# Recurrent heads, attention and Fourier mixing of a layer in one stage, with the recurrence's outputs in token rows

## The chip, the cores and the metric

The kernel runs on one core of one Trainium2 chip, in float32 throughout. The metric is the device time of one execution in microseconds (us). The matrix products are done by TensorE (PE in the profile; PEld is its weight load), element-wise work by VectorE (DVE), functions such as exp by ScalarE (ACT), and SyncE (SP) issues the weight transfers.

## The reference, cut to what matters

The network is two blocks. The first has two layers (`DEPTH = 2`) over 256 context and 256 latent tokens, width 1024; the second block is one layer and isn't touched by the change. A layer of the first block projects the normed tokens with one wide matrix and gives the columns to three branches, which are then merged:

```python
ul, uc = _split_cols(hl @ w_in), _split_cols(hc @ w_in)
ml_l, ml_c = _mlstm_branch(ul, uc, ml_gate_b, ml_head_g)
da_l, da_c = _diff_attn_branch(ul, uc, da_lam, da_head_g, cos, sin, lam_init, need_ctx)
yl = _merge(ml_l, da_l, _fourier(ul[8]), ul[9], w_br_ml, w_br_da, w_br_fn, w_out)
```

- The recurrence (mLSTM, 4 heads of 256): for both directions of time, with gate sums b and running maxima m, weights exp(min(bc + g, 0)) times q·k under a causal mask; the output of a direction is (weights @ v) / max(|sum of weights|, exp(-m)). The two directions are added, normed over the head's 256 channels, and multiplied with a gain and sigmoid(o).
- Differential attention (8 heads, a pair of them per 256 columns): two softmaxes per head with axial rotary positions, the second one subtracted with a factor, times v, normed per head.
- Fourier mixing (4 groups of 256 channels): the real part of a 2-D FFT over the tokens of a stream and the channels of a group:

```python
y = jnp.fft.fftn(z, axes=(1, 3), norm='ortho').real
```

In the second layer only the latent tokens' output is needed (`need_ctx` false), but keys and values of all tokens are.

## The kernel before, in words

Activations lie in SBUF as channels on partitions by tokens: `c.h` (normed) and `c.big` (the branches' outputs, 24 tiles of 128 channels). Weights come through a ring of four slots of 1 MB (1024 rows by 256 columns), each loaded by SyncE once the slot's last reader is through. PSUM has eight banks of 512 columns. The code is a row of stages (`Core.stage`). Within a stage each engine runs its own list and waits for others by semaphores; at a stage's end all engines meet (L228, `PEq L228` in the rows), and the semaphores are cleared. `full` is true in the first layer (`lo = 0`, all 512 tokens give outputs), false in the second (`lo = 256`).

Three functions make the branches of a layer, one after the other.

`mlstm` (L656) works head by head through `staggered` (L635): a stage of `projections` of a head and a stage of `core`, in turns, as a loop over three heads. `projections` (L763) multiplies K, Q and O with tokens last (16 multiplies of 8 by 8 tiles, L782), V with tokens first (L807), and beside them VectorE and ScalarE end the head before: |denominator|, maximum, reciprocal of 512 columns (L817, L818), product, sum over directions, squares, a multiply with ones over channels (L793), and the norm (L828 to L835). The first head's stage also holds `Gates`: gate products (L687), log-sigmoid, scans over tokens (L731 to L742), and the turned gate columns (L695). `core` (L875) does scores (L884), `A` on VectorE and ScalarE, and outputs with channels on partitions (L892): two multiplies with v and one with ones (the denominator) for each source tile.

`diff_attention` (L924) is a single stage, written out without loops. `steps` gives the order: while the items (a head by 128 tokens: scores L1046, exp L1101, `combine`, transposes L1059, output L1071, sums L1079) of a pair are worked off, the eight projection jobs of the next pair (L1015, L1021, with the quarter turns of the rotary positions, L1034) stand between them on TensorE. The first pair's jobs have no items beside them, and the last pair's items no jobs.

`fourier` (L1221) is a stage per group, three of them in a loop: projections with tokens last (L1236), a product with cosine and sine over channels (512 columns per token tile, L1243), a product over tokens (L1252), a copy into `c.big`.

After that comes `tail` (L1414 is its product), the same before and after.

Of the kernel before, what the change touches and what calls it, by code (L numbers as in the profile page):

```python
# [17 lines left out]
ALU = mybir.AluOpType  # L18
ACT = mybir.ActivationFunctionType
# [22 lines left out]
ML_COLUMNS, DA_COLUMNS, FN_COLUMNS = (COL_Q, COL_K, COL_O, COL_V), (COL_DAQ, COL_DAK, COL_DAV), (COL_FN,)  # L42
# [34 lines left out]
def _constant_columns():  # L77
    at = 0
    for name, width in (("ident", P), ("ones", P), ("upper", P), ("lower", P), ("turn", P), ("cos", NLAT), ("sin", NLAT),
                        ("dft", 2 * 3 * FN_C), ("pick", 4 * HG_SUB - 1), ("inner", HG_HEADS * NLAT), ("iota", PEER_K)):  # L80
        CST[name] = (at, width)
        at += width
    return at
# [25 lines left out]
class Core:  # L109


    def __init__(self, nc, ctx):
# [23 lines left out]
        def sem(name):  # L136
# [33 lines left out]
        self.decayed = sem("decayed")  # L170
        self.da_roped = sem("da_roped")
# [17 lines left out]
                     self.cleared, self.merged, self.averaged, self.inverted, self.rooted, self.scaled, self.moved, self.carried, self.paired, self.scored, self.apart,  # L189
                     self.decayed, self.da_roped, self.da_scored, self.da_max, self.da_exp, self.da_mixed, self.da_turned,  # L190
# [423 lines left out]
def over_turns(c, turns, columns, w_in, body, following):  # L614


    if not c.fetched:
        with c.stage() as block:
            @block.sync
            def _(sp):  # L620
                fetch(c, sp, head_loads(w_in, columns, 0))
    had = list(c.ahead_n)

    def wait_loaded(turn):
        return lambda engine, s: engine.wait_ge(c.ahead[s], turn * 16 + 16 * had[s])

    with c.nc.Fori(0, turns - 1) as turn:
        body(turn, wait_loaded(turn),
             lambda sp, wait_free=None: fetch(c, sp, head_loads(w_in, [col + CHUNK for col in columns], turn), wait_free))
    for s in range(len(columns)):  # L630
        c.ahead_n[s] = had[s] + turns - 1
    body(turns - 1, wait_loaded(turns - 1), lambda sp, wait_free=None: fetch(c, sp, following, wait_free))


def staggered(c, turns, columns, w_in, projections, core, following):  # L635


    if not c.fetched:
        with c.stage() as block:
            @block.sync  # L640
            def _(sp):
                fetch(c, sp, head_loads(w_in, columns, 0))
    had = list(c.ahead_n)

    projections(0, None, lambda engine, s: engine.wait_ge(c.ahead[s], 16 * had[s]))
    with c.nc.Fori(0, turns - 1) as turn:
        core(turn, lambda sp: fetch(c, sp, head_loads(w_in, [col + CHUNK for col in columns], turn)))
        projections(turn + 1, turn, lambda engine, s: engine.wait_ge(c.ahead[s], turn * 16 + 16 * (had[s] + 1)))
    for s in range(len(columns)):
        c.ahead_n[s] = had[s] + turns - 1  # L650
    core(turns - 1, lambda sp: fetch(c, sp, following))
    projections(None, turns - 1, None)


def mlstm(c, a, layer, w_in, full, following):
# [4 lines left out]
    lo = 0 if full else NCTX  # L660
    n = T - lo
    gcol, gh, headg, q, k, v, o, bc, A0, A1, E, den, hs, sq = c.carve(
        (2 * 4, 4), (2 * 4,), (2,), (2, T), (2, T), (4, ML_D), (2, T), (4, T), (4, T), (4, T), (2, T), (2, T), (2, T), (2, T))
    *_, gates, b, g, m, out_rows, wg, wg_apart = c.carve(
        (2 * 4, 4), (2 * 4,), (2,), (2, T), (2, T), (4, ML_D), (2, T), (4, T), (4, T), (2, T), (2, T), (2, T), (4, T), (KT, 16),
        (KT, P))
    logf, e = out_rows[:, 0:2], out_rows[:, 2:4]
    H = ML_HEADS

    class Gates:  # L670

        @staticmethod
        def sync(sp):
            sp.dma_start(wg, w_in[:, :, COL_GATE:COL_GATE + 16]).then_inc(c.stored, 16)

            sp.wait_ge(c.vec_out, 3)
            sp.wait_ge(c.act_out, 5)
            sp.dma_start(a["rows"], out_rows[0:H]).then_inc(c.stored, 16)  # L680
            sp.wait_ge(c.stored, 32)

        @staticmethod
        def products(pe):
            pe.wait_ge(c.drained, 1)
            for k in range(KT):
                last = pe.matmul(c.banks[7][:], wg_apart[:, k, :], c.h[:, k, :], start=k == 0, stop=k == KT - 1)  # L687
            last.then_inc(c.turned, 1)

        @staticmethod  # L690
        def turn(pe):
            pe.wait_ge(c.vec_out, 1)
            for d in range(2):
                for j in range(4):
                    last = pe.matmul(c.banks[6][:, (4 * d + j) * 4:(4 * d + j + 1) * 4], g[0:H, d, j * P:(j + 1) * P],  # L695
                                     c.constant("ident")[0:H, 0:H], start=True, stop=True)
            last.then_inc(c.turned, 1)
            pe.wait_ge(c.vec_out, 3)
# [2138 lines left out]
```

## Time and profile before

| | us |
|---|---|
| median of 3 runs | 3744.62 (3741.59 to 3747.61) |
| the profiled execution | 3744.39 |
| its span, first to last instruction | 3742.5 |
| TensorE busy | 3312.4 (89%) |
| VectorE busy | 1571.2 (42%) |
| ScalarE busy | 703.1 (19%) |

Shares of busy time are means over the whole span. The rows further down cut it into stretches. A float32 multiply shows as two records and two weight loads, so an "x32" is 16 multiplies. The granted clock is 1.0 at 2.4 GHz and 0.5 at 1.2 GHz; in a stretch it is the mean.

### The profile page before, as it was taken

The page shows a single profiled execution, that of the slowest core. Times are in us where ns is not written, and L with a number is a line of the kernel's source. Part 1 is how long each engine was busy: PE and PEld are TensorE (multiplying, and loading weights), DVE is VectorE, ACT ScalarE, POOL GpSimd, SP SyncE. Part 2 cuts the span into 40 slices and gives each one's busy share as a digit, 9 for nine tenths or more (in the row PEclk, how much of TensorE's full clock was granted, in tenths as well). Part 3 has the DMA queues.
Part 4 walks back from the last instruction along what each step waited for, and adds up shares of the span by engine and source line. Part 5 has one row for each costly group of instructions (what it writes and reads, how often), then busy time and mean ns, then how long its engine had stood idle before and what let it go on. Part 6 is the DMA issues. An engine that isn't in the chain of part 4 may idle for free. (4 is left out here: it accounts for less than half of the span.)

```text
span 3742.5 us, 33417 instructions
## 1 busy us (share of the span) xinstructions
PE 3312.4 (89%) x11640; PEld 2040.9 (55%) x11640; DVE 1571.2 (42%) x3286; ACT 703.1 (19%) x1639; POOL 426.7 (11%) x568
## 2 busy tenths in 40 slices
PE   6999799689999999998998978999989777787887
PEld 2555455344444844466766646888877663332332
DVE  1433345514432320002333443745127237777775
ACT  1211123300000200002111220010022104444443
POOL 0000000000000000000000000000000006665664
PEclk9999899799999999999999989999998789898989
DMA  5111110016433342232312203459432229999998
GB/s 183 68 56 56 66 58 23 1 34 224 148 133 124 137 155 79 76 99 79 113 67 80 67 1 121 153 179 373 150 124 68 68 71 424 422 416 411 410 423 351
DMA packets 280265, 588.69 MB, mean 157 GB/s; under 512 B 10888, under 2 KB 238984, under 8 KB 240584
## 3 DMA queue, kind: packets, MB, share of 16 engines
q0 software_dynamic: 44160, 338.97, 22.1%
q1 hardware_dynamic: 235984, 248.08, 19.9%
q8 instruction: 79, 1.29, 0.1%
q14 instruction: 42, 0.34, 0.0%
HBM read 585.91 MB, written 1.11 MB: 157 GB/s over the span
## 5 line engine op out<-in xcount | busy, mean ns | idle before, releaser
L1414 PE MATMUL banks<-normed,weight_ring 128*128 128x256 f32 (+1 forms) x2272 | 708.4, 474 | 9.1 <-ACT normed L1651 3.8
L1414 PEld LDWEIGHTS banks<-normed,weight_ring 128*128 128x128 f32 x2272 | 434.4, 191 | 281.1 <-issue 240.3
L1414 PE MATMUL banks<-branches,weight_ring 128*128 128x256 f32 (+1 forms) x1648 | 477.4, 451 | 0.0
L1414 PEld LDWEIGHTS banks<-branches,weight_ring 128*128 128x128 f32 x1648 | 313.1, 190 | 162.0 <-issue 133.9
L2677 PE MATMUL banks<-weight_ring,work 128*128 128x512 f32 x512 | 282.6, 711 | 127.5 <-ACT work L2642 127.5
L782 PE MATMUL banks<-normed,weight_ring 128*128 128x512 f32 (+1 forms) x768 | 282.6, 528 | 26.5 <-PEq L228 26.5
L2677 PEld LDWEIGHTS banks<-weight_ring,work 128*128 128x128 f32 x512 | 113.3, 229 | 296.2 <-issue 238.1
L2677 PE MATMUL banks<-work 128*128 128x512 f32 x512 | 229.4, 596 | 13.2 <-ACT work L2642 13.0
L546 DVE CUSTOM_DVE_ANT_0 work<-work 128x1024 f32<-128x1024 f32 x176 | 205.2, 1222 | 83.9 <-DMA work<-ada_turned 76.4
L782 PEld LDWEIGHTS banks<-normed,weight_ring 128*128 128x128 f32 x768 | 146.8, 192 | 157.2 <-issue 150.6
L1015 PE MATMUL banks<-normed,weight_ring 128*128 128x512 f32 (+1 forms) x512 | 205.7, 558 | 20.5 <-PEq L228 14.0
L2595 DVE CUSTOM_DVE_ANT_0 work<-work,branches 128x1024 f32<-128x1024 f32 x128 | 156.1, 1229 | 98.8 <-DMA work<-experts,work 95.7
L2677 PEld LDWEIGHTS banks<-work 128*128 128x128 f32 x512 | 95.3, 190 | 143.2 <-issue 104.0
L2570 POOL COPY work<-branches 128x1 uint32 (+1 forms) x256 | 114.8, 449 | 499.5 <-POOLq L228 466.5
L1015 PEld LDWEIGHTS banks<-normed,weight_ring 128*128 128x128 f32 x512 | 98.4, 196 | 122.8 <-issue 109.5
L2595 DVE CUSTOM_DVE_ANT_0 weight_ring<-weight_ring,branches 128x1024 f32<-128x1024 f32 x128 | 150.8, 1224 | 28.8 <-DMA weight_ring<-experts,work 22.8
L2574 POOL DMA_INDIRECT weight_ring<-experts,work x128 | 141.6, 1106 | 109.0 <-POOL work L2570 68.2
L2574 POOL DMA_INDIRECT work<-experts,work x128 | 141.8, 1108 | 101.9 <-POOL work L2570 80.4
L1551 DVE SCALAR_TENSOR_TENSOR stream<-banks,modulation,stream 128x256 f32<-128x256 f32 x48 | 22.7, 483 | 287.8 <-PE banks L1414 287.8
L1603 DVE TENSOR_TENSOR branches<-banks,branches 128x512 f32<-128x512 f32 (+1 forms) x44 | 24.1, 557 | 262.7 <-PE banks L1414 262.6
L1021 PE MATMUL banks<-weight_ring,normed 128*128 128x256 f32 x512 | 117.0, 383 | 4.2 <-DVE work L1144 4.2
L516 POOL DMA_DIRECT2D work<-condition_rows x2 | 1.2, 623 | 1040.5 <-issue 876.8
(408 smaller groups left out, 3739.3 us busy)
## 6 DMA issues: line engine op xcount, KB each, us to landing
weight_ring<-w_in SPq DMA_DIRECT2D x98, 1024.0 KB, 5.1
work<-ada_turned POOLq DMA_DIRECT2D x41, 1536.0 KB, 8.2
weight_ring<-w_ffn_in SPq DMA_DIRECT2D x44, 1024.0 KB, 5.1
weight_ring<-w_ffn_out SPq DMA_DIRECT2D x20, 1024.0 KB, 4.8
weight_ring<-w_out SPq DMA_DIRECT2D x12, 1024.0 KB, 4.8
weight_ring<-w_ada_first SPq DMA_DIRECT2D x8, 1024.0 KB, 8.7
work<-rows SPq DMA_DIRECT2D x8, 1024.0 KB, 4.7
weight_ring<-w_br_ml SPq DMA_DIRECT2D x8, 1024.0 KB, 5.3
```

Source lines behind the costliest of these rows:

```text
L516: pool.dma_start(self.rows[:, lo:hi, :], self.a["condition_rows"][lo:hi].partition_broadcast(P)).then_inc(c.rows_loaded, 16)
L546: last = dve.tensor_tensor_reduce(out=out, in0=slot[:, t, :], in1=self.rows[:, row, :], scale=1.0, scalar=0.0, op0=ALU.mult, op1=ALU.add, ...
L782: last = pe.matmul(c.banks[bank + half][:, 0:T - first], c.ring[:, s, kk, half * P:(half + 1) * P], c.h[:, kk, first:T], start=kk == 0, st ...
L1015: last = pe.matmul(bank[:, first:T], w[:, kk, half * P:(half + 1) * P], c.h[:, kk, first:T], start=kk == 0, stop=kk == KT - 1)
L1021: last = pe.matmul(bank[:, 0:2 * P], c.h[:, kk, j * P:(j + 1) * P], w[:, kk, :], start=kk == 0, stop=kk == KT - 1)
L1414: ins = pe.matmul(bank(i)[:, in_bank(p0, p1)], w[:, k - at, half * P:(half + 1) * P], source[:, k, cols(p0, p1)], start=k == 0, stop=k == ...
L1551: dve.scalar_tensor_tensor(out, bank(i + t)[:, in_bank(p, p + 1)], mod[:, gate_tile + t, parts[p][2]:parts[p][2] + 1], out, ALU.mult, ALU. ...
L1603: dve.tensor_tensor(out, bank(B_UP + NF + j)[:, in_bank(0, wide)], out, ALU.mult).then_inc(c.drained, 1)
L2570: pool.tensor_copy(place_u[:, r:r + 1], experts_u[:, bass.ds(u * K + (q * R + r), 1)]).then_inc(c.pool_done, 1)
L2574: pool.indirect_dma_start(out=fetched[r], out_offset=None, in_=a["experts"], in_offset=bass.IndirectOffsetOnAxis(ap=place_u[:, r:r + 1], a ...
L2595: dve.tensor_tensor_reduce(out=urows[r], in0=urows[r], in1=tokens[:, t, :], scale=1.0, scalar=0.0, op0=ALU.mult, op1=ALU.add, accum_out=do ...
L2677: last = pe.matmul(c.banks[2 * t + half][:], diag[:, r, :], vrows[r][:, half * 512:(half + 1) * 512], start=first, stop=isinstance(u, int) ...
```

## The change

The functions `over_turns`, `staggered`, `mlstm`, `diff_attention` and `fourier` go, and one function `branches` holds a single stage for all three branches of a layer, written out without loops. Its order on TensorE:

```python
for number in range(ML_JOBS):
    ml_job(0, number)
    if number == 1:
        gate_products()
    if number == 5:
        gate_turn()
for head in range(H):
    for step in range(ML_JOBS):
        if step < 4:
            ml_scores(head, step)
        if head + 1 < H:
            ml_job(head + 1, step)
        elif step < DA_JOBS:
            da_job(0, step)
        ml_after(head, step)
for item, kind, pair, number in da_steps():
    if item is not None and item < items:
        scores(item)
    if kind == "da":
        da_job(pair, number)
    if kind == "fn":
        fn_job(number)
    if item == items:
        turn_tokens(0)
    if item is not None:
        turn(item - 1)
    if item == items:
        turn_tokens(1)
    if item is not None:
        if ends_half(item - 2):
            output(item - 2)
        if item == items + 2:
            turn_channels(0)
        if ends_half(item - 3):
            sums(item - 3)
turn_tokens(2)
turn_channels(1)
turn_tokens(3)
turn_channels(2)
turn_channels(3)
```

A job is one bank: 0 to 5 are the halves of K, Q and O, 6 to 9 the four token tiles of V. All projections use banks 6 and 7 in turn and each job waits until the bank of two jobs before is copied; the recurrence's buffers are doubled. `ml_after` starts at step 3 (full) or 5 (`OUT_STEP`), and does the transposes of the tile before, then the outputs of this one. The recurrence's outputs are now in token rows, with the denominator as the 257th column of v:

```diff
-                for d in range(2):
-                    pe.wait_ge(c.vec_out, 4 * (d + 1))
-                    for bank, lhs in zip(outputs[d], (0, 1, None)):
-                        for i, (j, a0, a1) in enumerate(runs[d]):
-                            weights = c.constant("ones") if lhs is None else v[:, j, lhs * P:(lhs + 1) * P]
-                            pe.matmul(c.banks[bank][:, a0 - lo:a1 - lo], weights, A[d][:, j, a0:a1], start=i == 0,
-                                      stop=i == len(runs[d]) - 1)
+                for d in range(2):
+                    js = sources(d, t)
+                    for j in js:
+                        last = pe.matmul(c.banks[2 + 2 * (done % 2) + d][:, 0:V_W], A[d][:, j, t * P:(t + 1) * P], ml_v[buf][:, j, :],
+                                         start=j == js[0], stop=j == js[-1])
+                last.then_inc(c.ml_out, 1)
...
+    def sources(d, t):
+        if d == 0:
+            return list(range(t + 1))
+        return list(range(t, 2)) if t < 2 else [0, 1] + list(range(t, 4))
```

The norm of a tile is then a chain over per-token values, and two transposes bring it back to channels on partitions:

```diff
+            def join(head, x):
...
+                for d in range(2):
+                    chain.mark(dve.tensor_copy(its[:, d:d + 1], both[d][:, ML_D:V_W]))
+                chain.wait()
+                chain(dve.scalar_tensor_tensor(its[:, 0:2], its[:, 0:2], -1.0, its[:, 0:2], ALU.mult, ALU.max))
+                chain(dve.tensor_tensor(its[:, 0:2], its[:, 0:2], ecol[:, t:t + 5:4, head], ALU.max))
+                chain(dve.reciprocal(its[:, 2:4], its[:, 0:2]))
+                chain(dve.tensor_scalar(out, both[0][:, 0:ML_D], its[:, 2:3], None, ALU.mult))
+                dve.scalar_tensor_tensor(out, both[1][:, 0:ML_D], its[:, 3:4], out, ALU.mult, ALU.add).then_inc(c.ml_joined, 1)
...
+            def ml_square(head, x):
+                act.activation(squares, hs[done % 2], ACT.Square, accum_out=stat[:, done % 2, 4:5]).then_inc(c.ml_squared, 1)
...
+            def ml_invert(head, x):
+                chain(dve.tensor_scalar(its[:, 4:5], its[:, 4:5], 1.0 / ML_D, EPS, ALU.mult, ALU.add))
+                dve.reciprocal(its[:, 5:6], its[:, 4:5]).then_inc(c.ml_inverted, 1)
...
+            def ml_level(head, x):
+                act.activation(stat[:, done % 2, 6:7], stat[:, done % 2, 5:6], ACT.Sqrt).then_inc(c.ml_rooted, 1)
+                act.activation(hs[done % 2], hs[done % 2], ACT.Copy, scale=stat[:, done % 2, 6:7]).then_inc(c.ml_leveled, 1)
...
+                for half in range(2):
+                    last = pe.transpose(c.banks[2 + 2 * (done % 2)][:, half * P:(half + 1) * P],
+                                        hs[done % 2][:, half * P:(half + 1) * P], c.constant("ident"))
+                last.then_inc(c.ml_turned, 1)
```

`ml_place` then multiplies gain and sigmoid(o) into `c.big`. The gates' work is spread between the first head's copies on VectorE (`gate_fold`, `gate_sums` and `gate_maxima` ahead of copies 2, 3 and 4), and the turn (`gate_turn`) now also turns exp(-m) and waits for it (`gate_raised`), since the maximum is taken per token.

Fourier's projections are now tokens first (two token tiles to a bank), and the transforms come in the other order and use the symmetry of cosine and sine: over tokens with 129 cosine and 127 sine columns, over channels with 128 outputs of each kind, one more weight tile for the middle frequency, and the mirrored half made by adding and subtracting on VectorE (`fn_place`):

```diff
+                    for half in range(2):
+                        for kk in range(2):
+                            last = pe.matmul(c.banks[2 * (group % 2) + s][:, half * FN_C:(half + 1) * FN_C],
+                                             z[group][:, 2 * s + kk, half * P:(half + 1) * P], over_tokens[:, kk, :],
+                                             start=kk == 0, stop=kk == 1)
...
+                for half in range(2):
+                    last = pe.matmul(x_bank[:, used], over_channels[:, half, 0], uv[:, 2 * half, used], start=half == 0, stop=half == 1)
+                last.then_inc(c.fn_even, 1)
+                for half in range(2):
+                    pe.matmul(y_bank[:, used], over_channels[:, half, 1], uv[:, 2 * half + 1, used], start=half == 0, stop=False)
+                for half in range(2):
+                    last = pe.matmul(y_bank[:, used], over_channels[:, half, 2], uv[:, 2 * half, used], start=False, stop=half == 1)
```

`used` is 258 columns wide in the first layer and 129 in the second. ScalarE copies the token transform out of PSUM (`fn_spread`, four copies a group in the first layer) and lifts the even part (`fn_lift`). The constants change with it, and the rows of `w_br_fn` are put in the new channel order on the host when the inputs are packed. `ML_COLUMNS` has K before Q.

## Rows read from the trace of the kernel before

**Rows 1.** The page: the engine's busy time; weight loads of one line, mean ns.

```profile
PE 3312.4 (89%) x11640; PEld 2040.9 (55%) x11640; DVE 1571.2 (42%) x3286; ACT 703.1 (19%) x1639; POOL 426.7 (11%) x568
L782 PEld LDWEIGHTS banks<-normed,weight_ring 128*128 128x128 f32 x768 | 146.8, 192 | 157.2 <-issue 150.6
```

**Rows 2.** Windows: start:end, length, busy us by engine, granted clock, DMA.

```profile
74.70:142.85 68.15, 65.99 (x192) 35.80 (x193) 17.49 (x28) 12.42 (x14) 0.00 (x0) 0.97 0.06 18
142.85:385.17 242.32, 228.64 (x703) 129.27 (x703) 96.66 (x145) 34.27 (x55) 0.00 (x0) 0.99 0.19 65
385.17:478.37 93.20, 69.11 (x210) 39.91 (x211) 36.90 (x60) 10.04 (x16) 0.00 (x0) 0.85 0.20 68
478.37:675.43 197.06, 183.74 (x644) 105.16 (x643) 103.07 (x214) 56.81 (x136) 0.00 (x0) 0.98 0.12 38
675.43:874.95 199.52, 155.16 (x424) 81.53 (x423) 58.80 (x96) 23.76 (x55) 0.00 (x0) 0.87 0.11 37
1735.50:1795.82 60.32, 54.68 (x193) 37.15 (x193) 17.00 (x28) 11.93 (x14) 0.00 (x0) 0.93 0.07 20
1795.82:1978.69 182.87, 170.04 (x684) 129.04 (x685) 61.77 (x133) 27.00 (x55) 0.00 (x0) 0.98 0.25 86
1978.69:2048.43 69.74, 55.03 (x204) 40.31 (x204) 25.24 (x56) 8.07 (x16) 0.00 (x0) 0.88 0.27 91
2048.43:2195.17 146.74, 140.50 (x550) 93.75 (x549) 68.01 (x144) 37.59 (x76) 0.00 (x0) 1.00 0.16 51
2195.17:2318.72 123.55, 87.38 (x294) 58.60 (x293) 34.57 (x62) 15.05 (x32) 0.00 (x0) 0.83 0.16 52
```

**Rows 3.** TensorE's timeline over one head, first layer: start, us, instruction, [idle before].

```profile
164.04 13.99 PE L782 MATMUL banks<-normed,weight_ring 128*128 128x512 f32 x32 [1.06 <-PEq L228]
...
177.87 1.88 PE L793 MATMUL banks<-work,constants_sb 128*128 128x512 f32 x4
...
207.05 13.98 PE L807 MATMUL banks<-weight_ring,normed 128*128 128x256 f32 x64
223.16 5.41 PE L884 MATMUL banks<-work 128*128 128x512 f32 x16 [2.13 <-PEq L228]
230.03 4.58 PE L892 MATMUL banks<-work 128*128 128x512 f32 x16 [1.46 <-DVEq L918]
...
244.33 13.99 PE L782 MATMUL banks<-normed,weight_ring 128*128 128x512 f32 x32 [1.06 <-PEq L228]
```

**Rows 4.** TensorE's timeline: last head's end, last pair, first Fourier group, first layer.

```profile
421.05 3.78 PE L793 MATMUL banks<-work,constants_sb 128*128 128x512 f32 x4 [13.69 <-ACT work L860]
...
700.47 1.11 PE L1059 MATMUL banks<-constants_sb,work 128*128 128x128 f32 x4 [4.22 <-DVE work L1181]
...
756.57 7.13 PE L1243 MATMUL banks<-constants_sb,work 128*128 128x512 f32 x16 [0.78 <-DVE work L1262]
```

**Rows 5.** VectorE's timeline in the last pair, first layer.

```profile
702.97 0.17 DVE L1175 RECIPROCAL work<-work 128x2 f32<-128x2 f32 x1 [1.09 <-ACT work L1101]
...
703.75 0.48 DVE L1181 SCALAR_TENSOR_TENSOR work<-work 128x256 f32<-128x256 f32 x1
...
733.79 3.35 DVE L1189 RECIPROCAL work<-work 128x512 f32<-128x512 f32 x1
```

**Rows 6.** ScalarE's timeline: an attention item (first layer), the gates (second layer).

```profile
705.54 0.47 ACT L1101 ACTIVATE work<-banks,work 128x256 f32<-128x256 f32 x1
...
1765.11 1.28 ACT L709 ACT_TABLE_LOAD   x1
1766.40 1.06 ACT L709 ACTIVATE work<-work 4x1024 f32<-4x1024 f32 x1
```

**Rows 7.** Second layer's gates: gate product and V (TensorE), the denominators' floor (ScalarE).

```profile
1751.80 7.03 PE L687 MATMUL banks<-normed,work 128*128 128x512 f32 x16
...
1778.33 15.62 PE L807 MATMUL banks<-weight_ring,normed 128*128 128x256 f32 x64 [3.08 <-DVE work L748]
...
1778.03 1.06 ACT L712 ACTIVATE work<-work 4x1024 f32<-4x1024 f32 x1 [9.27 <-DVEq L746]
```

More of the change, by code:

```diff
@@ L611, in head_loads @@
     return [w_in[:, :, bass.ds(turn * CHUNK + col, CHUNK)] for col in columns]
[L614 to L632, printed above, removed]
@@ L635, in staggered @@
[L635 to L652, printed above, removed]
@@ L923, in diff_attention, with at @@
-def diff_attention(c, a, layer, w_in, full, following):
-    lo = 0 if full else NCTX
-    n = T - lo
-    PAIRS = DA_HEADS // 2
-    tiles = [t for t in range(4) if t * P >= lo]
+    first = lo // NCTX
+    tiles = [t for t in range(4) if t * P >= lo]
+    streams = range(first, 2)
+    H, PAIRS, FG = ML_HEADS, DA_HEADS // 2, FN_GROUPS
+    had = list(c.ahead_n)
+    def at(lo_, *shape):
+        view = c.work[:, lo_:lo_ + math.prod(shape)]
+        if len(shape) == 2:
+            view = view.rearrange("p (a b) -> p a b", b=shape[1])
+        elif len(shape) == 3:
+            view = view.rearrange("p (a b c) -> p a b c", b=shape[1], c=shape[2])
+        return view
@@ new lines, in proj_bank, with jobs_to_end_of @@
+    def proj_bank(tile):
+        return c.banks[6 + tile % 2]
+    pieces = ([("ml", h, i) for h in range(H) for i in range(4)] + [("da", pair, i) for pair in range(PAIRS) for i in range(3)]
+              + [("fn", g_, 0) for g_ in range(FG)])
+    def jobs_to_end_of(piece):
+        kind, turn, i = pieces[piece]
+        if kind == "ml":
+            return turn * ML_JOBS + (2, 4, 6, 10)[i]
+        if kind == "da":
+            return DA_FIRST + turn * DA_JOBS + (2, 4, 8)[i]
+        return FN_FIRST + len(streams) * (turn + 1)
@@ L1033, in quarter_turn @@
+            def quarter_turn(pair, which, source, x):
+                tile = DA_TILE_0 + pair * DA_TILES + which
+                free_bank(tile)
+                wait_copied(pe, DA_TILE_0 + pair * DA_TILES + source)
                 for half in range(2):
@@ L1196, in scale, with fn_copy @@
                                          ).then_inc(c.da_scaled, 1)
-            before = None
-            for item, pair, number in steps():
+            def fn_copy(number):
+                group, s = number // len(streams), streams[number % len(streams)]
+                dve.wait_ge(c.product, FN_FIRST + number + 1)
+                dve.tensor_copy(z[group][:, 2 * s:2 * s + 2, :],
+                                proj_bank(FN_TILE_0 + number).rearrange("p (j n) -> p j n", j=2)).then_inc(c.copied, 1)
@@ L1200, in _ @@
+            before = None, 0, 0
+            for item, kind, pair, number in da_steps():
                 if item is not None and ends_half(item - 4):
```

887 lines of the change are left out of this document (507 added, 380 removed).

## The prediction

> **What bounds the kernel now.** I read the page's engine shares first: TensorE is busy for 89% of the span [rows 1], so either its work or its idle time has to shrink. Next the windows: I cut both layers' branch stages where TensorE's rows change kind [rows 2]. In each layer the five stretches are the recurrence's opening, its heads 1 to 3, its last head with the first attention pair's projections, the attention pairs under the next pair's projections, and the last pair with Fourier. The ten add up to 1383.5 us, with TensorE busy for 1210.3. Nothing else in the kernel is touched, so 2359.0 us stay. The reader is to see how unlike the five are. While projections stand between attention items TensorE has 183.7 of 197.1 us and 140.5 of 146.7 (layer 2); at the last head, and at the last pair with Fourier, it has 69.1 of 93.2, 155.2 of 199.5, 55.0 of 69.7 and 87.4 of 123.6, at a granted clock of 0.83 to 0.88. VectorE's busiest stretch is half full. So matmul columns bound nearly all of it, and a few chains through VectorE and ScalarE bound the ends.
>
> **Price of a matmul.** A projection of 16 multiplies of 512 columns takes 13.99 us, one of 32 multiplies of 256 columns 13.98 (each multiply is two records) [rows 3]: 0.437 us per 256 columns. The copies' bank handshake is hidden in both.
>
> **1. Recurrence, heads 1 to 3 of a layer.** Before, one head lasts 80.3 us (164.04 to 244.33) [rows 3]: projections 55.3 without the sum of squares, scores 5.4, outputs 13.2 (230.03 to 243.27), sum of squares 1.7, the rest (about 4.7) waits at two stage ends and for the first outputs. After, outputs are in token rows: per direction and 128 tokens one multiply of 257 columns for each source tile. Counted from `sources` that is 10 + 10 = 20, or 8.8 us; the 3840 columns in each of two directions go down to 2570, the denominators being column 257. The 512-wide ones multiply goes too. Added are two transposes per tile; four took 1.11 us at half clock [rows 4], so two take about 0.3, 1.3 per head.
> Next, waits. TensorE does scores, a 7.0 us (K, Q, O) or 3.5 us (V) job of the next head, then the transposes of the tile whose output it made a step earlier, then the next output. The chain that the transposes wait for is: `join`, five small VectorE operations at 0.17, two at about 0.45 and gaps, 1.9 us; ScalarE's square with its accumulator read, 0.6; `ml_invert` 0.4; a square root and a scaled copy, 0.7 [rows 5, 6]. With hand-overs that is 3.8 us, and 4.6 where the square-root table is loaded beside `ml_invert`. I bound it by 3.5 and by 7.7 (the 4.2 us that TensorE waited for a like attention chain [rows 4] on top of 3.5). I take 4.6, as its pieces have rows. In layer 1 tiles 0 and 1 are under 7.0 us jobs (no wait), 2 and 3 under V jobs: 1.1 + 0.3 of wait. Per head 55.3 + 5.2 + 8.8 + 1.3 + 1.4 = 72.0; for three 216, against 242.3: **-26**. VectorE has some 27 us of work per 72, as three 3.35 us reciprocals of 512 columns [rows 5] go with the channel-row form.
> Layer 2 in the same way: projections 41.6, scores 3.4, 14 multiplies of 257 columns 6.1, transposes 0.6, both tiles under V jobs 1.4: 53.1. Three are 159.3 against 182.9: **-23.6**.
>
> Each first square root after an exponential or a sigmoid needs a table. In the gate's chain a load of 1.28 us is followed at once by its activation (1765.11, then 1766.40) [rows 6]. The Trainium skill, ScalarE: Activation LUTs, "What ACT_TABLE_LOAD costs", gives 2.66 us for a switch, since about 1.38 us of drain come on top. The trace doesn't agree: there is no room for that drain between the two rows. By the page one chain in each of eight heads would be 1.4 us longer and the end 11 us later.
>
> **2. Opening.** The gate product and its scans now run beside the copies, and 16 tiny multiplies more (as many as took 1.9 us) turn the denominators' floor. In layer 1 the scans end under Q and O, so +1.9, less 0.6 at the missing stage end: **+1.3**. In layer 2 Q and O last 14 us only. Today V starts 19.5 us after the gate product (1758.83 to 1778.33) [rows 7]. Now the turn waits for the floor too (its exponential ended at 1779.11 [rows 7]), and the copy of Q stands behind the scans on VectorE: +20.6, turn to +22.7: 3.2 later, less 0.6: **+2.6**. Behind that wait stand the V jobs; SyncE's row loads wait there also, but the weights for the next head are due 14 us later.
>
> **3. Last head.** Today its normalisation is alone (TensorE waits 13.7 us for `ones` [rows 4]), and the first attention pair's projections follow alone. After, those eight jobs (45.0 us) stand between its steps: 45.0 + scores 5.2 + outputs 8.8 + transposes 1.3, waits 3.0 (all four tiles are under 3.5 us V jobs, and VectorE has a rope before one join), 0.8 for the last `ml_place` before the first attention scores: 64.1 against 93.2: **-29**. Layer 2: 36.7 + 3.4 + 6.1 + 0.6 + 1.4 + 0.8 = 49.0 against 69.7: **-20.7**.
>
> **4. Middle pairs.** Same order, same banks, same copies: 197.1 and 146.7 stay. Cost bounded by 0 and by their idle time, 13 and 6 us either way; I take 0.
>
> **5. Last pair and Fourier.** Fourier's projections (56 us in layer 1, 28 in layer 2) now stand under the last pair's items, as attention's do in the middle pairs: a middle pair keeps TensorE busy for 61.2 us (183.7 by three), 44 of them jobs and quarter turns, so 55.8 + 17.3 = 73.1. Then the transforms: over tokens 2 streams of 4 multiplies of 256 columns, 3.5 us per group (before 16 passes, 7.13 us [rows 4]); over channels 6 of 258 columns, 2.6 (before as many columns again as over tokens). All this comes after the last item, with no projection to cover it: 4 x 3.5, 4 x 2.6, the last turn, output and sums 4.1, a wait of 2.6 at group 1 for the last head's average, reciprocal (3.35 [rows 5]), root and scale, the last group's four VectorE operations 2.3 and the stage end 1.3: 34.7. 107.8 against 199.5: **-91.7**. Layer 2: 28 of projections, 10.1 of items (46.8 a middle pair less 36.7 of jobs) and some 2 of waits, 40.2; 4 x 1.7; the channel transform has 129 columns, less than one weight load (0.19 us [rows 1]) per pass, so between 1.3 and 2.3 us a group, I take 1.8, 4 x 1.8; turn, output, sums 2.7; waits 1.9 and 0.4; end 2.8: 62.0 against 123.6: **-61.5**.
>
> **Sum.** Layer 1: -26.3 + 1.3 - 29.1 - 91.7 = -145.8. Layer 2: -23.6 + 2.6 - 20.7 - 61.5 = -103.2. Together -249. The profiled execution took 3744.4 us (span 3742.5 and 1.9 around it), which is the runs' median of 3744.6 within 0.3. 3744.4 - 249 = 3495.4, so **3495 us**. Cross-check by kind: columns removed are worth about 77 us, stretches at 0.83 to 0.88 of the clock some 30, idle time the other 140; 173 us are idle in rows 2, so some 35 remain.
>
> **Rivals.**
> *A. Longer chains.* Every tile's chain takes the upper bound of 7.7 us, 3.5 over mine: the 18 tiles under V jobs wait that much more (six in heads 1 to 3 of layer 1, four in its last head, eight in layer 2), and six under 7.0 us jobs 0.7: +67, 3562 us. For it: TensorE's 4.22 us wait for VectorE in the last pair [rows 4]. Against: that chain holds 512-column operations and a reciprocal, mine 256-column ones.
> *B. Fourier hides badly.* If the three transform groups at the end run one after another, each waiting for ScalarE's spreads (1.6 us), lift and VectorE's placing (2.3), that is 4 us for each of 4 groups, twice, +32; with the middle pairs 10 us worse: 3538 us. Against: two banks' worth of groups are in flight.
> *C. Less left over.* With denser matmuls the clock stays at 2.4 GHz throughout (0.97 to 0.99 now) and the waits of parts 1 and 3 vanish: -20, 3476 us.
> *D. Slower: the clock.* The new order puts a short wait at each step; if these keep the clock at 1.2 GHz for much of the two stages, they lose what they gain. Some 1100 us of TensorE work at full clock are left in them; 1100 x (1/x - 1) reaches 249 at a mean clock of x = 0.815, and at 0.71 the time is about 3744 + 200 = 3944. For it: stretches with long waits have 0.83 to 0.88 [rows 2]. Against: with waits of 1 to 2 us the middle heads and pairs have 0.98 and more. The Trainium skill, TensorE: Matmul & The Clock Gate, "HAM oscillation — how this bites in real kernels", tells of a loop that falls back to half clock at each wait; by it D would be the case if the waits here were as long.
> *E. It doesn't do what it says.* The loops become straight code; if instruction supply held TensorE, gaps named issue would stand before MATMUL. The attention pairs are straight code already and show none, so only the columns (77) and half of the idle time would come: 3600.
>
> **Chances.** Forecast 68%, A 8%, B 12%, C 9%, D 1%, E 2%. A measurement of this kernel can't tell 0.2% (7.5 us) from no change. Faster by over 0.2%: 0.98; within: 0.01; slower: 0.01. The range goes from C's side to past B: 3470 to 3550.
>
> **What would show it.** Window of heads 1 to 3 in layer 1 near 216 us, TensorE idle about 1.4 per head, at the transposes under V jobs; one step of the last head without a gap over 2 us; no idle stretch over 3 us before Fourier's transforms, and one of 2 to 3 in them; about 108 and 62 us from the last pair's first scores to the next stage; in layer 2 a gap of some 10 us at the gate's turn, which is new. I am wrong if TensorE's clock is under 0.95 in the stages, if its transposes wait over 4 us each, or if the middle pairs change length.

## The result

The changed kernel takes 3511.78 us (median of 4 runs, 3507.74 to 3514.94) against 3743.11 for the kernel before on the same chip: 0.938 of its time, 95% interval 0.9364 to 0.9396. The forecast was 3495, its range 3470 to 3550. The profiled execution took 3509.25 us, its span is 3507.4.

Windows of the kernel after, cut as [rows 2] (same columns). The first row, the seventh and the last two are code that the change doesn't touch; the ten others are the ten stretches, in the order of the table below.

```profile
0.00:75.14 75.14, 41.41 (x160) 16.41 (x161) 13.46 (x34) 18.64 (x38) 0.21 (x4) 0.88 0.68 225
75.14:145.66 70.52, 69.25 (x209) 38.74 (x209) 18.18 (x32) 13.50 (x14) 0.00 (x0) 0.95 0.19 62
145.66:360.14 214.48, 210.62 (x672) 124.72 (x673) 68.89 (x227) 51.44 (x96) 0.00 (x0) 1.00 0.20 64
360.14:421.61 61.47, 58.78 (x201) 36.74 (x199) 27.86 (x89) 10.71 (x26) 0.00 (x0) 1.00 0.17 52
421.61:620.74 199.13, 185.26 (x642) 105.75 (x642) 102.72 (x213) 56.88 (x137) 0.00 (x0) 0.97 0.15 48
620.74:729.69 108.95, 102.06 (x472) 82.61 (x471) 51.26 (x94) 30.71 (x75) 0.00 (x0) 1.00 0.16 49
729.69:1592.11 862.42, 854.66 (x2384) 453.38 (x2385) 229.88 (x401) 63.70 (x120) 16.13 (x30) 1.00 0.38 131
1592.11:1655.19 63.08, 57.30 (x208) 39.30 (x209) 17.62 (x32) 12.96 (x14) 0.00 (x0) 0.91 0.22 68
1655.19:1814.46 159.27, 155.42 (x624) 116.85 (x625) 44.49 (x149) 29.05 (x63) 0.00 (x0) 1.00 0.27 86
1814.46:1863.20 48.74, 46.76 (x186) 34.21 (x184) 19.91 (x63) 7.53 (x18) 0.00 (x0) 1.00 0.21 66
1863.20:2009.99 146.79, 140.46 (x549) 93.75 (x549) 67.66 (x143) 37.69 (x77) 0.00 (x0) 1.00 0.21 65
2009.99:2075.58 65.59, 56.50 (x278) 45.81 (x277) 32.15 (x64) 18.70 (x44) 0.00 (x0) 0.97 0.26 81
2075.58:2752.32 676.74, 625.50 (x3616) 545.50 (x3617) 307.63 (x635) 91.66 (x181) 12.14 (x22) 0.94 0.47 160
2752.32:3507.40 755.08, 589.87 (x1392) 277.89 (x1392) 501.46 (x1256) 291.14 (x838) 406.50 (x512) 0.88 0.89 363
```

| stretch | before | forecast | after |
|---|---|---|---|
| layer 1, opening | 68.2 | 69.5 | 70.5 |
| heads 1 to 3 | 242.3 | 216 | 214.5 |
| last head | 93.2 | 64.1 | 61.5 |
| middle pairs | 197.1 | 197.1 | 199.1 |
| last pair, Fourier | 199.5 | 107.8 | 109.0 |
| layer 2, opening | 60.3 | 62.9 | 63.1 |
| heads 1 to 3 | 182.9 | 159.3 | 159.3 |
| last head | 69.7 | 49.0 | 48.7 |
| middle pairs | 146.7 | 146.7 | 146.8 |
| last pair, Fourier | 123.6 | 62.0 | 65.6 |
| the ten | 1383.5 | 1134.5 | 1138.0 |
| all other code | 2359.0 | 2359.0 | 2369.4 |

The ten stretches lost 245.5 us, where 249 were forecast. TensorE is busy for 1082.4 of the 1138.0 us. 10.4 us were given back in code that is the same in both kernels, 8.0 of it in the last two rows, which in the kernel before were these:

```profile
2318.72:2994.25 675.53, 628.51 (x3616) 548.39 (x3617) 307.56 (x635) 91.82 (x181) 12.15 (x22) 0.93 0.46 162
2994.25:3742.50 748.25, 581.22 (x1392) 273.52 (x1392) 500.82 (x1256) 291.81 (x838) 398.23 (x512) 0.90 0.89 366
```

TensorE's timeline in the kernel after, first head of layer 1, as [rows 3]: scores are L895, outputs L908, transposes L916, projections L849 and L858.

```profile
178.36 1.47 PE L908 MATMUL banks<-work 128*128 128x257 f32 x6
179.66 7.03 PE L849 MATMUL banks<-normed,weight_ring 128*128 128x512 f32 x16
186.53 0.38 PE L916 MATMUL banks<-constants_sb,work 128*128 128x128 f32 x2
...
195.13 3.21 PE L908 MATMUL banks<-work 128*128 128x257 f32 x14
198.18 3.62 PE L858 MATMUL banks<-weight_ring,normed 128*128 128x256 f32 x16
202.89 0.44 PE L916 MATMUL banks<-constants_sb,work 128*128 128x128 f32 x2 [1.09 <-ACT work L1124]
...
210.02 0.44 PE L916 MATMUL banks<-constants_sb,work 128*128 128x128 f32 x2 [0.20 <-ACT work L1124]
```

The transposes at 186.53 wait for nothing, since a 7.0 us job stood ahead of them; at 202.89 a V job of 3.6 us did, and the rest of the chain shows, 1.09 us with the square-root table to load, 0.20 without at 210.02. The forecast had 1.1 and 0.3.

TensorE in layer 2, at the gates and in the last pair (and, of ScalarE, the exponential of the denominators' floor):

```profile
1630.37 5.88 PE L849 MATMUL banks<-normed,weight_ring 128*128 128x256 f32 x16 [4.50 <-DVE work L1258]
1634.88 1.06 ACT L1097 ACTIVATE work<-work 4x1024 f32<-4x1024 f32 x1 [9.40 <-DVEq L1241]
1636.18 3.73 PE L883 MATMUL banks<-constants_sb,work 4*128 4x4 f32 x32
...
2048.92 1.89 PE L985 MATMUL banks<-merged,work 128*128 128x256 f32 x8
...
2058.50 3.43 PE L985 MATMUL banks<-merged,work 128*128 128x256 f32 x8 [3.36 <-DVE branches L1383]
...
2067.06 0.68 PE L1031 MATMUL banks<-work,constants_sb 128*128 128x129 f32 x4 [1.64 <-DVE branches L1383]
```

The wait of 4.50 us is for the copy of Q's second half, queued behind gate sums on VectorE. The wait of 3.36 us is larger than the forecast had there: the last output needs the bank that the previous head's scaling frees, and the four items of this pair in layer 2 didn't cover that chain. The output behind it then takes 3.43 us, where the same eight records took 1.89 at 2048.92.

### The profile page after: what moved, and what is told of

Its sections match the earlier page's. It is cut to its first block and busy times, and to the rows that moved or that the text cites. A ratio compares the mean times of both kernels' runs of the same rounds, so it can differ in the third digit from the quotient of the medians.

```text
span 3507.4 us, 32781 instructions
## 1 busy us (share of the span) xinstructions
PE 3193.9 (91%) x11584; PEld 2011.7 (57%) x11584; DVE 1503.2 (43%) x3428; ACT 734.3 (21%) x1736; POOL 435.0 (12%) x568
## 5 line engine op out<-in xcount | busy, mean ns | idle before, releaser
L849 PE MATMUL banks<-normed,weight_ring 128*128 128x512 f32 (+1 forms) x1280 | 491.6, 540 | 31.8 <-PEq L266 20.5
L2876 PE MATMUL banks<-weight_ring,work 128*128 128x512 f32 x512 | 290.7, 730 | 127.9 <-ACT work L2841 127.9
L849 PEld LDWEIGHTS banks<-normed,weight_ring 128*128 128x128 f32 x1280 | 246.2, 194 | 256.7 <-issue 245.1
L858 PE MATMUL banks<-weight_ring,normed 128*128 128x256 f32 x1408 | 319.3, 383 | 4.6 <-DVE work L1332 4.6
L858 PEld LDWEIGHTS banks<-weight_ring,normed 128*128 128x128 f32 x1408 | 265.4, 191 | 58.9 <-issue 23.9
L2769 POOL COPY work<-branches 128x1 uint32 (+1 forms) x256 | 136.2, 532 | 496.0 <-POOLq L266 464.5
L2773 POOL DMA_INDIRECT weight_ring<-experts,work x128 | 132.0, 1031 | 108.9 <-POOL work L2769 67.3
L2834 ACT ACTIVATE work<-work 128x1 f32<-128x1 f32 x256 | 51.8, 202 | 326.0 <-DVE work L2794 320.8
L1358 DVE TENSOR_REDUCE work<-banks 128x2 f32<-128x1024 f32 (+1 forms) x48 | 50.2, 1046 | 155.1 <-PE banks L960 155.1
```

Of the source, the lines that this page charges most:

```text
L849: last = pe.matmul(proj_bank(tile)[:, since:T], w[:, kk, half * P:(half + 1) * P], c.h[:, kk, since:T], start=kk == 0, stop=kk == KT - 1)
L858: last = pe.matmul(proj_bank(tile)[:, x * CHUNK:(x + 1) * CHUNK], c.h[:, kk, j * P:(j + 1) * P], w[:, kk, :], start=kk == 0, stop=kk == KT ...
L1358: chain(dve.reduce_max(its[:, 6:8], c.psum[:, u:u + 2, 0:keys(i)], AX.X))
L2769: pool.tensor_copy(place_u[:, r:r + 1], experts_u[:, bass.ds(u * K + (q * R + r), 1)]).then_inc(c.pool_done, 1)
L2773: pool.indirect_dma_start(out=fetched[r], out_offset=None, in_=a["experts"], in_offset=bass.IndirectOffsetOnAxis(ap=place_u[:, r:r + 1], a ...
L2834: act.activation(gl[:, r:r + 1], dot[:, r:r + 1], ACT.Gelu).then_inc(c.act_done, 1)
```

## The experiments

The times are medians; "after" is the changed kernel, which is the base of every edit. They ran on other chips than the result above, so the ratio to the kernel before on the same chip is given too.

### Fourier's projections behind the last pair (fn_after)

```diff
-                elif full:
-                    yield item, "fn", 0, number
                 else:
-                    yield item, "fn" if number % 2 == 0 else None, 0, number // 2
+                    yield item, None, 0, 0
+        for number in range(FN_JOBS):
+            yield None, "fn", 0, number
```

> Fourier's projections stand behind the last attention pair's items, not between them. My theory (cover: items and projections add up once they aren't interleaved, since an item waits for VectorE and ScalarE): in the first layer the eight items alone took 49 us before, plus 56 us of projections, against 74.2 us from the pair's first scores to the last projection now: +31; second layer 25 + 28 against 40.4: +12.5. Together about +43 us, near 3555. Rival (the last pair was only moved, its waits come back elsewhere, so that cover is worth little and the gain is Fourier's fewer columns): under +15 us.

3567.98 us, ratio 0.9523 (0.9503 to 0.9543). Windows of the pairs with Fourier, first layer then second, here and in the kernel after:

```profile
420.80:755.59 334.79, 298.94 (x1113) 194.99 (x1113) 154.44 (x306) 86.70 (x211) 0.00 (x0) 0.94 0.14 44
1892.93:2128.07 235.14, 206.55 (x824) 144.95 (x825) 99.82 (x206) 55.93 (x121) 0.00 (x0) 0.93 0.20 63
```

```profile
421.61:729.69 308.08, 287.32 (x1113) 188.36 (x1113) 153.98 (x306) 87.59 (x211) 0.00 (x0) 0.98 0.15 48
1863.20:2075.58 212.38, 196.96 (x825) 139.56 (x825) 99.81 (x207) 56.38 (x121) 0.00 (x0) 0.99 0.22 70
```

+26.7 and +22.8 us, for the 31 and 12.5 expected: the cover (multiplies of TensorE that stand between the steps of a chain, so that the chain runs beside them) is real, and the rival is out. The matmuls are the same 1113 and 825 records (one is missing from a trace), yet TensorE is busy 11.6 and 9.6 us longer, at a lower clock. So a part of what cover gives is the clock, which the expectation had left out.

### The last head with nothing beside it (head_alone)

```diff
-                    elif step < DA_JOBS:
-                        da_job(0, step)
                     ml_after(head, step)
+            for number in range(DA_JOBS):
+                da_job(0, number)
```

and the copies on VectorE likewise.

> The last head of each layer runs without the first attention pair's projections between its steps; they follow. Cover theory: alone, a head of the first layer takes about 5 us to its first weights, outputs 8.6, four chains of 4 to 4.6 us, transposes 1.3: 32 us against 16.5 now (61.5 less 45 of projections): +15; second layer +12. Together +27 us, 3539. Rival (token rows alone shortened the head's end, cover adds little): under +10 us.

3553.95 us, ratio 0.9494 (0.9474 to 0.9514). The heads' window of layer 1 grew from 276.0 to 301.1 us (the pairs' shrank by 2.1), that of layer 2 from 208.0 to 225.0: +23 and +17. Again more than 15 and 12. In layer 1 TensorE idles for 15 us more than in the kernel after, about what was expected in all, and is busy for 10.0 us more (279.4 for 269.4) in the same multiplies. Its timeline, at the last head of layer 1 and at that of layer 2:

```profile
373.38 0.69 PE L916 MATMUL banks<-constants_sb,work 128*128 128x128 f32 x2 [5.23 <-ACT work L1124]
373.86 2.78 PE L908 MATMUL banks<-work 128*128 128x257 f32 x6
380.29 0.69 PE L916 MATMUL banks<-constants_sb,work 128*128 128x128 f32 x2 [3.65 <-ACT work L1124]
...
390.15 5.67 PE L908 MATMUL banks<-work 128*128 128x257 f32 x14
...
1854.34 0.69 PE L916 MATMUL banks<-constants_sb,work 128*128 128x128 f32 x2 [4.54 <-ACT work L1124]
```

This is the chain by itself: 3.65 us (3.8 was priced), and 4.54 with the table load (4.6). The 5.23 us hold 0.7 more, since VectorE was still mixing the head's last weights: its `join` of this tile starts at 368.87, 0.7 us behind the outputs' end, and that of the next tile at 376.68, at once. The six and fourteen records of outputs take 2.78 and 5.67 us, where the kernel after has 1.47 and 3.21: half clock.

### Nothing beside anything (nothing_beside)

The two edits, and in the head loop all of a head's core before the next head's ten jobs, on TensorE, VectorE and ScalarE:

```diff
-                    if head + 1 < H:
-                        ml_job(head + 1, step)
                     ml_after(head, step)
+                if head + 1 < H:
+                    for step in range(ML_JOBS):
+                        ml_job(head + 1, step)
```

> As both before, and heads 1 to 3 too: first a head's core with nothing beside it, then the next head's ten projection jobs; token rows, symmetric Fourier and the single stage stay. Cover theory: +16 us for each of three heads in the first layer and +13 in the second, 87, with 27 and 43 of the other two: +157 us, 3669, so two thirds of the gain are cover and some 75 us remain for fewer columns and stage ends. Rival (the clock): waits of 4 us at each tile keep TensorE's granted clock below 0.9 in both stages, which adds 100 us and more: 3770 or above, slower than the kernel before.

3721.4 us, ratio 0.9936 (0.9917 to 0.9956). Windows of the heads, first and second layer:

```profile
147.12:524.39 377.27, 306.13 (x873) 180.84 (x873) 95.79 (x315) 50.72 (x113) 0.00 (x0) 0.88 0.14 45
1778.97:2048.81 269.84, 225.67 (x808) 162.06 (x808) 63.25 (x211) 36.68 (x81) 0.00 (x0) 0.90 0.20 63
```

+210 us, between the two theories. Against the kernel after (269.4 and 202.2 us busy, at 1.00), TensorE is busy 36.7 and 23.5 us longer for the same multiplies; with the pairs' windows it comes to 74 us, with the openings' to 80, of the 210.7 by which the stages grew. The other 131 are idle time, for which the expectation had 157. So the clock is over a third of what cover gives, but doesn't make the kernel slower than before. What is left against the kernel before, 0.6%, is a net of several terms and not the price of fewer columns: the kernel before ran a head's norm beside the next head's projections, which this one doesn't, and behind the stages this one took 1441.7 us in its profile, for 1423.8.

### Fourier's transforms twice (doubled)

```diff
-                    for half in range(2):
+                    for half in (0, 1, 0, 1):
```

and the same for the three products over channels.

> Both Fourier transforms' multiplies are issued twice (same result), about as many as the full-size transforms had over channels and tokens. If their columns are on the path: first layer 4 x (3.45 + 2.6) = 24, second 4 x (1.73 + 1.35) = 12, less 7 us of waits at the end that they would now cover: +29 us, 3541. Rival (the end is held by VectorE and ScalarE, reciprocals, spreads and placing, not by TensorE): under +12 us.

3545.97 us, ratio 0.9467 (0.9449 to 0.9486). The pairs' windows are 329.8 and 224.5 us, +21.8 and +12.1, together 33.8 for 29: the columns are on the path, and the waits were covered rather more in layer 1 (the 2.26 us one is gone) than in layer 2. As the full-size transforms had these columns once more, the symmetric form is worth about as much.

### Each job waits for the bank just before it (one_bank)

```diff
-            def free_bank(tile):
-                if tile >= 2:
-                    wait_copied(pe, tile - 2)
+            def free_bank(tile, back=1):
+                if tile >= back:
+                    wait_copied(pe, tile - back)
```

(quarter turns keep 2).

> Each projection job waits until the bank of the job just before it is copied, instead of the one before that: a short wait of TensorE at nearly each step. By the waits alone: where an item's maxima stand ahead of the copy on VectorE about 2.2 us per item step (32 in the first layer, 16 in the second), and 0.7 to 0.9 us at jobs with little between them (some 70): about +160 us, 3672, with the granted clock staying above 0.95. Rival (the clock, the slower side of the forecast): short waits at every step bring the mean clock of both stages under 0.9, +120 us on top: 3790, slower than before.

3657.45 us, ratio 0.9772 (0.9757 to 0.9787). Windows: heads and pairs of layer 1.

```profile
151.88:433.19 281.31, 272.67 (x873) 160.63 (x873) 96.68 (x316) 62.15 (x122) 0.00 (x0) 1.00 0.19 60
433.19:815.14 381.95, 309.28 (x1113) 201.33 (x1113) 154.31 (x306) 87.92 (x211) 0.00 (x0) 0.93 0.12 39
```

+146 us for the 160 expected; the three windows of each layer (opening, heads, pairs) grew by 148.8. In layer 1 the pairs lose 73.9 us, 22.0 of it busy time, at a clock of 0.93; the heads lose 5.4 at 1.00. The expectation had the clock above 0.95 throughout, which the pairs miss. TensorE's records in the pairs show waits of up to 3.0 us, each for a copy. Many short waits don't bring rival D about.

### The opening in another order (gates_later)

```diff
                 if number == 2:
                     gate_fold()
-                if number == 3:
-                    gate_sums()
-                if number == 4:
-                    gate_maxima()
                 ml_copy(0, number)
+                if number == 3:
+                    gate_sums()
+                    gate_maxima()
...
-            gate_floor()
             open_gate(0, 0)
             open_gate(0, 1)
+            gate_floor()
...
-                if number == 5:
+                if number == 8:
                     gate_turn()
```

> Opening only: the copies of Q ahead of the gate scans on VectorE, sigmoid of O ahead of the floor on ScalarE, and the gate turn after three V jobs. My theory (the 4.5 us idle before the second O job in the second layer is the copy queued behind the scans): second layer's opening 63.1 to 58.6 us, first layer's unchanged at 70.5; 3507. Rival (the scans' own end is what is waited for, so the wait moves to the turn or to the first scores): opening stays within 1 us of 63.

3502.23 us, ratio 0.9371 (0.9354 to 0.9388). TensorE in layer 2's opening:

```profile
1614.38 13.98 PE L849 MATMUL banks<-normed,weight_ring 128*128 128x256 f32 x64
1628.19 10.52 PE L858 MATMUL banks<-weight_ring,normed 128*128 128x256 f32 x48
1638.64 3.73 PE L883 MATMUL banks<-constants_sb,work 4*128 4x4 f32 x32
```

The opening is 56.1 us against 63.1: -7.0. With the copy ahead of the sums, and the turn behind three V jobs, nothing is waited for. The wait of the kernel after was the copy's place in the queue; the run moves the turn too, so it doesn't say how much the copy alone would give (in the kernel after the floor was ready at 1635.94 only, 0.2 us before TensorE came to the turn). The 2.5 us beyond the wait's 4.5 are mostly the job behind it, 5.88 us at 1630.37 where 3.6 is the full-clock time. By the whole times the two kernels' intervals overlap, so the gain rests on the window.

### The square-root table early (table_early)

```diff
+                act.activation(stat[:, done % 2, 7:8], c.constant("ones")[:, 0:1], ACT.Sqrt)
                 act.wait_ge(c.ml_joined, done + 1)
```

> A one-element square root ahead of each tile's wait loads the table while ScalarE is idle. If the waits of 1.1 to 1.4 us before the transposes, one per head, are the table load beside the inversion: each falls to 0.2, -0.9 x 8 = -7 us, 3504. Rival (a switch also drains ScalarE for 1.4 us, or the extra loads delay sigmoid and exponentials): no change or slower by up to 10 us.

3510.03 us, ratio 0.9381 (0.9368 to 0.9393). TensorE's second V job and transposes of the first head:

```profile
196.77 3.62 PE L858 MATMUL banks<-weight_ring,normed 128*128 128x256 f32 x16
200.58 0.44 PE L916 MATMUL banks<-constants_sb,work 128*128 128x128 f32 x2 [0.19 <-ACT work L1125]
```

1.09 us became 0.19; the heads' windows are 2.7 and 3.6 us shorter, 6.3 for the 7 expected. In the whole time that isn't seen: 3510.03 for the 3504 expected, which lies below all five executions (3507.38 to 3514.00), since the code behind the stages took 1435.1 us in the profile, against 1431.8.

### Both (gates_and_table)

> Both of the foregoing edits. If they are independent the sum, -12 us: 3500, ratio to the changed kernel 0.9967; heads 1 to 3 of the second layer from 159.3 to 156.6 us and its opening at 58.6.

3502.33 us, ratio 0.9358 (0.9345 to 0.9371). The parts add in the windows (layer 2: 56.0 and 204.5 us). The profiled execution took 3511.33 us nevertheless: behind the branch stages it needed 1447.6 us.

### What lies behind the stages (before_again, before_third, after_again)

The kernels before and after again, without an edit.

> The kernel before once more, for a second profile: everything behind the branch stages is the same code in both kernels, yet lasted 1423.8 us in the first profile of before and 1431.8 after. If that difference is scatter between executions: between 1424 and 1440. If the change causes it: within 2 us of 1423.8.

> The changed kernel once more: ten stretches of the branch stages within 4 us of 1138, the code behind them 1430 to 1440 us if the change makes it longer, down to 1424 if it is scatter.

> As before_again, a third profile of the kernel before: behind the branch stages 1424 to 1440 us if scatter, 1422 to 1426 if not.

3742.49, 3514.31 and 3749.78 us. From the end of the second layer's stages to the last instruction the kernel before took 1423.8, 1424.9 and 1427.2 us in three profiles; the kernel after 1431.8 and 1437.2, and its eight variants 1430.7 to 1447.6. The groups don't overlap, so the +10 us aren't scatter, though the kernel before scatters more than expected: 1427.2 lies outside the 1422 to 1426 set for "not scatter". The pages differ in the landing of weights, even before the first stage that the change touches. In before_third:

```profile
weight_ring<-w_ffn_in SPq DMA_DIRECT2D x44, 1024.0 KB, 5.1
weight_ring<-w_ada_first SPq DMA_DIRECT2D x8, 1024.0 KB, 8.8
```

In after_again (the columns are count, size, median us from issue to landing):

```profile
weight_ring<-w_ffn_in SPq DMA_DIRECT2D x44, 1024.0 KB, 5.6
weight_ring<-w_ada_first SPq DMA_DIRECT2D x8, 1024.0 KB, 9.5
```

### SBUF tensors where they were (placed)

The edits of gates_and_table, and

```diff
-        self.cst = sb("constants_sb", [P, N_CST])
+        self.cst = sb("constants_sb", [P, N_CST + 56])
...
-            sp.dma_start(c.cst[:], a["constants"])
+            sp.dma_start(c.cst[:, 0:N_CST], a["constants"])
```

> The two opening and table edits together, and 56 unused columns behind the constants in SBUF alone (the table in HBM and its transfer keep their size). The change made the constants 254 columns shorter and so moved every SBUF tensor: the weight ring starts at 131328 bytes in the kernel before, a multiple of 256, and at 130336 after, a multiple of 32 only; here at 130560, a multiple of 256 again. Theory (placement): weight transfers of 1 MB land in 4.7 to 4.8 us again where they took 5.2 to 5.5 (w_out), the first weights in 8.7 and not 9.4, and the code behind the branch stages takes 1423 to 1428 us instead of 1431 to 1448: about 3492 us. Rival (placement in HBM, or the longer straight code, slows the transfers): landings and the 1431 to 1448 us stay, 3502 us.

3492.77 us (3487.02 to 3496.09), ratio 0.9331 (0.9314 to 0.9347): the fastest version. The code behind the stages takes 1422.9 us, below all ten profiles with the other placement. Its page:

```profile
weight_ring<-w_ffn_in SPq DMA_DIRECT2D x44, 1024.0 KB, 5.1
weight_ring<-w_out SPq DMA_DIRECT2D x12, 1024.0 KB, 5.2
weight_ring<-w_ada_first SPq DMA_DIRECT2D x8, 1024.0 KB, 8.6
```

The first weights and `w_ffn_in` land as in the kernel before; `w_out` doesn't (4.8 before), nor does `w_br_da` (5.3 for 4.8). The HBM side and the code kept their form, so it is where the tensors start in SBUF that costs the 10 us. The 1422.9 is from one profile, of the fastest of five executions (3487.02), and the 1447.6 of gates_and_table is from its slowest; the medians of the two are 9.6 us apart, no execution of one reaches the other's, and the intervals of their ratios just touch.

In all 14 profiles the code behind the stages has the same 5008 records on TensorE. With the tensors as in the kernel before (four profiles) they are busy for 1206.8 to 1211.7 us, with the others (ten) for 1212.0 to 1230.6; in the mean that is 9.5 of the 11.9 us between the two groups, at a granted clock of 0.91 to 0.92 against 0.90 to 0.91. So most of the loss is TensorE taking longer for the same work, and not idle time. How the starts, the slower landings and the lower clock hang together is not shown.

## Why the prediction was right, step by step

- **Price of a matmul.** Held: seven multiplies of 257 columns (14 records) take 3.05 us from their start to that of the next job (195.13 to 198.18), so 0.44 each; two transposes take 0.21 to 0.27 in the same way, for the 0.3 priced.
- **1. Heads 1 to 3.** 214.5 and 159.3 us for 216 and 159.3. head_alone shows the chain bare at 3.65 us (3.8 priced) and 4.54 with the table (4.6 priced: of the load's 1.28 us some 0.9 show), table_early that the table is what made the 1.09 us waits. The two table rows had decided against the drain that the Trainium skill, ScalarE: Activation LUTs, "What ACT_TABLE_LOAD costs", adds to a load; with it these waits would be 2.5, so the trace bears the row out.
- **2. Opening.** 70.5 and 63.1 for 69.5 and 62.9. The place of the wait was wrong, and its size: not some 10 us at the turn (it waited for nothing at 1636.18) but 4.5 at the job before it, whose bank's copy was queued behind the gate sums. The start of the turn was right all the same, since the floor was ready 20.4 us after the gate product (20.6 in the sum). Behind it two errors cancel, which is luck: the turn took 3.7 us, where the sum had about 2, and V took 14.1, where it had taken 15.6 before.
- **3. Last head.** 61.5 and 48.7 for 64.1 and 49.0. The waits under the rope and the V jobs were 2.0 us, not 3.0; 1.4 us of it the one behind VectorE's rope. Most of the rest is busy time, 58.8 us where the terms add up to 60.3.
- **4. Middle pairs.** 199.1 and 146.8 for 197.1 and 146.7. The 2.0 us of layer 1 are outside what "same order, same banks, same copies" allows: TensorE was busy for 1.5 us longer, at 0.97 for 0.98.
- **5. Last pair and Fourier.** 109.0 and 65.6 for 107.8 and 62.0. In layer 1 the wait at group 1 was 2.26 us for 2.6. In layer 2 the waits behind the last projection were 3.36 and 1.64 us, for 1.9 and 0.4, and the output behind the first ran at half clock (3.43 us for 1.89); the channel transforms gave some back, 1.34 us a group (2070.20 to 2071.54) for the 1.8 taken. fn_after and doubled show the two halves of the step by themselves: cover 49 us, transform columns 34.
- **The rest.** "Nothing else in the kernel is touched, so 2359.0 us stay" failed: +10.4 us. This is most of the 17 us by which 3495 was low. The change shortened the constants by 254 columns, and every SBUF tensor moved with them; placed takes the 10 us back. The stretches give 3.5 of the 17, and the median lies 2.5 above the profiled execution.
- **Cross-check by kind.** It had put 30 us on the clock and 77 on columns. The busy time of the ten stretches fell by 128, from 1210.3 to 1082.4, so their sum was low by 21. Which of the two terms was too small isn't separated; that the clock can cost more than I gave it is seen in nothing_beside, with 80 us of busy time for the same multiplies.
- **Rivals.** A: the upper bound of 7.7 us a chain isn't reached even without cover (at most 5.23). B: the groups at the end ran without a wait but the one at group 1. C: the clock did reach 1.00 in six of the ten stretches, but the waits at the transposes stayed. D: taken furthest in nothing_beside, 0.88 to 0.90, never 0.815. E: no wait of a matmul for instructions is in the timeline; the straight code ran as the loops did.
- **Signs.** Of the signs of being wrong two showed faintly: the opening of layer 2 had a clock of 0.91 (0.93 before), and the middle pairs of layer 1 changed by the 2.0 us. No transpose of the recurrence waited for over 1.4 us.

## What to carry to other kernels

Where one engine bounds and its waits come from chains through others, price the chain from single rows and compare it with the length of the work that stands before its consumer; here that gave stretches within 4 us. Add the clock to what a wait costs: the multiplies that follow it may run at half speed. And when a resident table changes its size, keep the start of the buffers that transfers write to, or measure it: the code far from the change isn't safe.

## What the runs showed of the hardware

- The start of SBUF tensors matters in this kernel. Three starts of the weight ring were run: at 130336 bytes, a multiple of 32 but not of 64, the same code takes 1431 to 1448 us (ten profiles); at 131328 and at 130560, multiples of 256, 1423 to 1427 (four). What lies between isn't measured.
- The clock can fall without a gap. In gates_later the first layer's 16 turns of 4 columns took 5.01 us, and the V job behind them 5.73 where 3.6 is the full-clock time, although TensorE had been busy without a break for over 13 us before them, at a granted clock of 1.00. Timeline, and windows before and from the turns on:

```profile
122.70 10.52 PE L858 MATMUL banks<-weight_ring,normed 128*128 128x256 f32 x48
133.15 5.01 PE L883 MATMUL banks<-constants_sb,work 4*128 4x4 f32 x32
138.09 5.73 PE L858 MATMUL banks<-weight_ring,normed 128*128 128x256 f32 x16
```

```profile
120.00:133.15 13.15, 13.15 (x55) 10.07 (x53) 0.87 (x3) 2.94 (x3) 0.00 (x0) 1.00 0.54 162
133.15:143.80 10.65, 10.65 (x49) 9.30 (x48) 0.42 (x1) 0.00 (x0) 0.00 (x0) 0.68 0.00 0
```

In the kernel after the turns of layer 1 took 3.73 us, without a gap before them, and the four V jobs behind them 15.77, at a granted clock of 0.77 in their first 7.4 us; in layer 2 the V jobs took 14.08. In layer 2 of gates_later the turns took 3.73 us and the job behind them 3.72. So it doesn't happen each time, and no run here shows what decides it. The Trainium skill, TensorE: Matmul & The Clock Gate, "What's actually happening", says that activity releases the throttle. The rows behind waits agree; that the clock falls in a stream without a gap doesn't follow from that sentence.
